# A thirteen-slot ring of expert weights, rows fetched per expert, and the smallest expert last, in a hybrid SSD/GLA/MoE layer

## The reference

```
scores = sigmoid(h2 @ w_router); biased = scores + router_bias
best   = argmax over the 4 groups of the sum of their two highest biased scores
idx    = top 2 of the 16 experts, inside the best group only
comb   = scores at idx, scaled to the sum 1, zero elsewhere
y_moe  = sum over e of comb[:, e] * ((silu(h2 @ wg[e]) * (h2 @ wu[e])) @ wd[e])
x = x + g2 * y_moe ;  y = rms_norm(x, final_norm_w)
```

## Time and profile before

| | |
|---|---|
| median of 3 runs | 1006.31 us |
| the profiled execution's own time | 1004.06 us |
| its span, first to last instruction | 1002.3 us |
| TensorE, VectorE, ScalarE, GpSimd busy | 94%, 44%, 23%, 14% |
| moved by DMA in all | 236.98 MB, mean 236 GB/s |
| GB/s in slices 31 to 38 of 40 | 387 419 419 420 417 420 420 421 |

### The profile page before, as it was taken

The page is one execution under the profiler, slowest core; times in us unless marked ns, Lnnn a source line. Parts: engine busy times, 40 slices in busy tenths (PEclk is TensorE's granted clock), DMA queues, the critical chain, the costliest instruction groups (busy, mean ns, idle before and its releaser), DMA issues.

```text
span 1002.3 us, 18836 instructions
## 1 busy us (share of the span) xinstructions
PE 944.0 (94%) x7702; PEld 659.7 (66%) x7702; DVE 441.4 (44%) x1094; ACT 233.2 (23%) x461; POOL 145.3 (14%) x236
## 2 busy tenths in 40 slices
PE   5999999999999999999999999999899988797895
PEld 2667666666666666666666777767599856564671
DVE  3221234676346986656641531134643342322316
ACT  2231222243263322232252300002231110110013
POOL 0000232343020343322300000011200000000010
PEclk9999999999999999999999999999999999899997
DMA  9943344564455655665443533342579999999973
GB/s 376 392 165 126 127 169 143 197 225 162 161 193 197 255 196 179 227 218 202 159 172 126 224 122 127 126 168 98 214 291 387 419 419 420 417 420 420 421 281 118
DMA packets 46541, 236.98 MB, mean 236 GB/s; under 512 B 6672, under 2 KB 10352, under 8 KB 23152
## 3 DMA queue, kind: packets, MB, share of 16 engines
q1 hardware_dynamic: 44480, 229.83, 59.7%
q0 software_dynamic: 1520, 5.34, 1.6%
q10 hardware_dynamic: 448, 0.50, 0.1%
HBM read 212.34 MB, written 23.31 MB: 235 GB/s over the span
## 4 chain that ended last, share of the span: by engine, by line
PE 73%; DMA 15%; DVE 6%; issue 2%; ACT 2%; SPq 1%; POOL 0%; POOLq 0%; DVEq 0%
PE pjB L884 15%; PE pjA L884 15%; DMA ring<-in_w 8%; PE pjA L1282 7%; PE pjB L1282 7%; DMA bp<-in_w 4%; PE states L1456 4%; PE states L1468 3%; PE states L1459 2%; DMA yd<-hF 2%; PE states L893 1%; PE bank L1019 1%; PE states L1261 1%; PE states L1019 1%; PE bank L1248 1%
## 5 line engine op out<-in xcount | busy, mean ns | idle before, releaser
L884 PE MATMUL pjA<-hF,ring 128*128 128x320 f32 x608 | 171.9, 436 | 0.5 <-ACT regA L1719 0.5
L884 PE MATMUL pjB<-hF,ring 128*128 128x320 f32 x608 | 171.8, 435 | 0.0
L884 PEld LDWEIGHTS pjA<-hF,ring 128*128 128x128 f32 x608 | 113.2, 190 | 50.7 <-issue 7.0
L884 PEld LDWEIGHTS pjB<-hF,ring 128*128 128x128 f32 x608 | 113.3, 190 | 48.6 <-issue 4.7
L1456 PE MATMUL states<-ring,oF 128*32 128x128 f32 x720 | 80.5, 273 | 2.1 <-DMA ring<-in_w 1.7
L1456 PEld LDWEIGHTS states<-ring,oF 128*32 128x32 f32 x720 | 78.0, 110 | 5.5 <-issue 2.7
L1459 PE MATMUL states<-ring,oF 128*32 128x384 f32 x720 | 80.7, 491 | 0.0
L2764 DVE TENSOR_TENSOR oF<-oF,states 128x256 f32<-128x256 f32 (+1 forms) x15 | 7.2, 483 | 139.9 <-PE states L1468 70.4
L2470 DVE TENSOR_TENSOR G<-G 128x320 f32<-128x320 f32 x32 | 47.1, 1510 | 0.0
L2076 POOL TENSOR_TENSOR G<-regA,G 128x128 f32<-128x128 f32 (+1 forms) x32 | 19.0, 594 | 192.3 <-ACT G L1775 192.3
L2173 POOL DMA_DIRECT2D yd<-hF x1 | 0.6, 640 | 244.2 <-DVE hF L2755 244.2
(11 more groups left out here) (565 smaller groups left out, 1518.2 us busy)
## 6 DMA issues: line engine op xcount, KB each, us to landing
ring<-in_w SPq DMA_DIRECT2D x144, 1024.0 KB, 8.5
rF<-in_w SPq DMA_DIRECT2D x11, 1024.0 KB, 18.6
bcF<-in_w SPq DMA_DIRECT2D x11, 1024.0 KB, 20.6
bp<-in_w SPq DMA_DIRECT2D x10, 1024.0 KB, 19.0
G<-in_ss SPq DMA_DIRECT2D x16, 512.0 KB, 4.7
out_ss_new<-G SPq DMA_DIRECT2D x16, 512.0 KB, 2.9
G<-csd SPq DMA_DIRECT2D x16, 320.0 KB, 3.5
G<-in_sg SPq DMA_DIRECT2D x4, 1024.0 KB, 6.4
```

Source lines behind the costliest of these rows:

```text
L884: mm = pe.matmul(pj[g % 2][:, 0:T], w[:, k, half * P:half * P + P], hF[:, k, :], start=(k == 0), stop=(k == KT - 1))
```

## The change

**Ring.** `SLOTS` goes from R + 3 to R + 7. The four new slots lie in xsF (two) and regA (two). Eleven chunks (`KNOWN`) are those of places 0 and 1 whose experts are known beforehand, without the last; they are asked for before the branch, number 11 in the branch as soon as the residual has been read out of regA, number 12 after the transposes of place 0's rows. Chunk order changes: gate and up of place 1 come before down of place 0.

**Rows per expert.** The 40 transposes of all rows, their copies and ScalarE's copy by offset go. SP loads each place's rows from `xd` to one of two buffers (`rows_in`), three places ahead, TensorE turns them (`turn_rows`, 8 transposes) between gate/up of place p and down of place p-1, ScalarE and VectorE copy 4 of the 8 tiles each. The `yd` writes move from SP to ScalarE's queue.

**Places.** `FULL_AT` is now 0, 1, 4, 6, 8, 10; `TINY_AT` 5, 9, 13 are places of up to 32 tokens, with `tiled_tiny` streaming 128 columns through each column group; the others hold 64, the last one too, which now gets the smallest expert. By the counts above places 0 to 15 hold 57, 31, 47, 44, 77, 27, 59, 40, 55, 25, 50, 36, 29, 18, 29 and 16 tokens.

**End.** The last expert's 16 tokens are finished apart: for up to 64 rows TensorE picks gate, residual and the other expert's contribution (`each_row`), VectorE and ScalarE norm them, and POOL scatters the finished rows over the ordinary ones in the output, after those have landed. For tokens 0 to 255 the residual is added by POOL, not VectorE.

The tables:

```diff
-SLOTS = R + 3
+SLOTS = R + 7
+KNOWN = R + 5
...
-FULL_AT = (0, 1, 2, 5, 8, 11, 14, 15)
-FIXED_AT = (0, 1, E - 1)
...
+FULL_AT = (0, 1, 4, 6, 8, 10)
+TINY_AT = (5, 9, 13)
+FIXED_AT = (0, 1)
```

SP, in the layer's last loads and then in the branch:

```diff
+                    sp.wait_ge(s_used, C_OUT)
+                    load_extra(3)
+                    load_extra(4)
...
+                sp.wait_ge(s_tm, 6)
+                sp.dma_start(slot(KNOWN), d["w"][chunk_row(*SEQ[KNOWN])]).then_inc(slot_ready(KNOWN)[0], 16)
                 sp.wait_ge(s_xd, 16 * 6)
-                sp.dma_start(xs01[:, 0, :], d["xd"][0:P, :]).then_inc(s_xe[0], 16)
-                sp.dma_start(xs01[:, 1, :], d["xd"][P:2 * P, :]).then_inc(s_xe[1], 16)
-                sp.wait_ge(s_oss, GH + 1)
-                sp.dma_start(hT, d["xd"][2 * P:XROWS, :].rearrange("(a p) c -> p a c", p=P)).then_inc(s_xe[1], 16)
...
+                rows_in(1)
+                sp.wait_ge(s_oss, GH + 2)
+                sp.dma_start(slot(KNOWN + 1), d["w"][weight_row(2) + SEQ[KNOWN + 1][1]]).then_inc(slot_ready(KNOWN + 1)[0], 16)
+                rows_in(2)
+                refill(0, 0, 4)
...
+                for p in range(3, LAST):
+                    refill(p, 0, 4)
+                    if p + 3 < E:
+                        rows_in(p + 3)
+                    refill(p - 1, 4, 6)
```

TensorE:

```diff
+                gate_up(0)
+                turn_rows(1)
+                gate_up(1)
+                turn_rows(2)
+                down(0)
+                turn_rows(3)
+                down(1)
+                gate_up(2)
+                for p in range(3, LAST):
+                    gate_up(p)
+                    turn_rows(p + 1)
...
+                    down(p - 1)
+                down(LAST - 1)
+                gate_up(LAST)
+                turn_act()
+                base_rows(0)
+                down(LAST)
+                base_rows(1)
+                base_rows(2).then_inc(s_gw, 1)
+                row_sums()
```

GpSimd, behind the six gathers:

```diff
+                for t in range(2):
+                    pool.wait_ge(s_gm, t + 1)
+                    pool.tensor_tensor(hT[:, t, :], hT[:, t, :], xT[:, t, :], ALU.add).then_inc(s_x3, 1)
+                pool.wait_ge(s_tix, 2)
+                pool.wait_ge(s_f, 4)
+                pool.wait_ge(s_out, 16 * 4)
+                pool.indirect_dma_start(out=d["yrows"], out_offset=bass.IndirectOffsetOnAxis(ap=tix[:, 0:1], axis=0),
+                                        in_=zF_, in_offset=None).then_inc(s_last, 16)
```

VectorE, the end:

```diff
+                summed(0).then_inc(s_gm, 1)
+                gated_up(LAST)
+                turned_last()
+                summed(1).then_inc(s_gm, 1)
+                cm(summed(2))
                 cm.wait()
...
+                dve.tensor_tensor(hT[0:NSAMP, 2, :], hT[0:NSAMP, 2, :], xT[0:NSAMP, 2, :], ALU.add).then_inc(s_base, 1)
+                final(0, 0, y2)
+                dve.wait_ge(s_gwc, 3)
+                weighted_half(0)
+                weighted_half(1)
+                final(1, 1, y2)
+                dve.wait_ge(s_zl, 2)
+                dve.wait_ge(s_gw, 2)
+                dve.tensor_tensor(zL, zL, b[4][:, :], ALU.add).then_inc(s_zl, 2)
+                final(2, 2, y2)
+                dve.wait_ge(s_zq, 2)
+                dve.reciprocal(zs[:, 1:2], zs[:, 1:2]).then_inc(s_frc, 1)
+                dve.wait_ge(s_frc, 4)
+                dve.scalar_tensor_tensor(zF_, zL, zs[:, 1:2], w2, ALU.mult, ALU.mult).then_inc(s_f, 1)
```

More of the change, by code:

```diff
@@ L821, in refills @@
                 of, row = None, None
[L822 to L827, removed]
+                for j in range(j0, j1):
+                    m = seq_of(p, j)
+                    if m in NEXT:
+                        q, i = SEQ[NEXT[m]]
+                        if q != of:
+                            of, row = q, weight_row(q)
+                        sp.wait_ge(s_used, C_MOE + m + 1)
+                        sp.dma_start(slot(NEXT[m]), d["w"][row + i]).then_inc(slot_ready(NEXT[m])[0], 16)
@@ L1470, in tiled_small, with tiled_tiny, gate_up @@
                 return mm
-            def gate_up(e, v, full=True):
-                he = heF[:, v]
+            def tiled_tiny(bank, rows, w, first, last):
+                for q in range(4):
+                    at = QUAD * q
+                    mm = pe.matmul(bank[at:at + QUAD, 0:P], rows(0), w[:, P * q:P * q + P], start=first, stop=last,
+                                   tile_position=(0, at), skip_group_check=True)
+                return mm
+            def gate_up(p):
+                he, tiles = heF[:, p % 2], tiled if p in FULL_AT else tiled_tiny if p in TINY_AT else tiled_small
+                if p:
+                    pe.wait_ge(s_hea, p)
+                    pe.wait_ge(s_heb, p)
                 for part, used in ((0, s_esg), (1, s_eac)):
-                    if not (isinstance(e, int) and e == 0):
-                        pe.wait_ge(used, e + 0)
+                    if p:
+                        pe.wait_ge(used, p)
                     for half in range(2):
-                        w = moe_chunk(pe, e, 2 * part + half)
+                        w = moe_chunk(pe, p, 2 * part + half)
                         for k in range(4):
@@ new lines, in base_rows, with row_sums @@
+                return mm
+            def row_sums():
+                pe.wait_ge(s_zq, 1)
+                for h in range(2):
+                    for half in range(2):
+                        mm = pe.matmul(b[0][SMALL * h:SMALL * h + SMALL, 0:1], ident[:, SMALL * half:SMALL * half + SMALL],
+                                       zs[:, 0:1], start=(half == 0), stop=(half == 1), tile_position=(0, SMALL * h),
+                                       skip_group_check=True)
+                mm.then_inc(s_gw, 1)
@@ L1599, in up @@
                     for part, used in ((0, s_sg), (1, s_au)):
-                        w = [moe_chunk(pe, e, 2 * part + half) for half in range(2)]
+                        w = [dense_chunk(pe, e, 2 * part + half) for half in range(2)]
                         for f in range(4):
```

676 lines of the change are left out of this document (333 added, 343 removed).

## The result

The changed kernel takes 1020.82 us in the median of 4 runs (1017.0 to 1024.55); the kernel before, measured again beside it, 1007.08 (1005.38 to 1008.71). The ratio is 1.0136, with a 95% interval of 1.0092 to 1.0181: slower by 13.7 us. The prediction was 995.5, a miss of 25.3 us. The profiled execution took 1017.0 us, its span is 1015.0.

The account below looks back on a forecast made before the run. The DMA weight stream was taken as the bound: last weight 10.0 us earlier, end 31.2 us instead of 31.9, together -10.7 us. From 1004.06 that makes 993.4; with 2.25 to the median, 995.5 was predicted, range 985 to 1003.

Parts of the forecast that it names:

- What must flow: Weight stream: chunks 11 to 95, fetched rows and results sum to 97.65 MB, 242.3 us at 0.403 MB/us.
- Start: Start of the branch's weight stream: chunk 11 issued at 715.8, data from 717.1 (715.7 to 719.6), 1 us of idle.
- the prediction's own signs of being wrong: Wrong if the stream doesn't start before 718 or the end behind the last gather is not 20 to 22 us.
- The two extra known chunks at nothing: Before the branch: two more 1 MB loads before 690 us cost nothing; without that cover 2 x 2.6 us.
- Rate and last weight: Weight stream: at 0.403 MB/us the last weight lands at 960.4, 10.0 us earlier.
- rival 1: Weight stream: engines stay even at 0.414 MB/us and TensorE's clock stays up, 986.6 us; chance 0.17.
- TensorE as cover: Weight stream: TensorE's work takes 220 of 242 us, so it stays beside the stream.
- Place 14's result: ScalarE's queue: issued at 947.1, 7.8 us and half a us for the second, landed at 955.3, gathers from 956.0.
- Rival 2: Place 14's result is no faster on ScalarE's queue, gathers 8.3 to 9.8 us later, about 1003.5 us; chance 0.11.
- The end: From the last weight to the end: 31.2 us instead of 31.9, output landed 987.5, scatter 991.4, span 991.6.
- The rule on the shared port: Residual additions at the end: POOL and VectorE pass each other; by the skill's contrary rule 4.3 us more, 999.8.
- Rival 3: Weight stream: TensorE becomes the bound as its clock falls; 1019 us with a quarter at half clock; chance 0.06.

Follow-up runs that it names:

- quarters: Changed kernel, but each place's rows are fetched as quarters of 256 columns over all 128 partitions, with 2 transposes per 32 rows: 994.1 us.
- low64: Changed kernel, but for places 5 to 15 each fetch brings 64 rows of 4 KB into partitions 0 to 63: 1021.8 us.
- mid64: Changed kernel, but for places 5 to 15 each fetch brings 64 rows of 4 KB into partitions 32 to 95: 997.0 us.
- q_ring11: Kernel with quarter rows fetched over 128 partitions, but a ring of 11 slots, without the two in regA: 994.9 us.
- q_ysp: Kernel with quarter rows over 128 partitions, but all places' results return to SP's queue, each behind the refills that follow its place: 999.3 us.
- q_vadd: Kernel with quarter rows over 128 partitions, but the end's residual additions of groups 0 and 1 go from GpSimd to VectorE: 994.5 us.
- all128: Changed kernel, but every fetch brings 128 whole rows of 4 KB into all 128 partitions, whatever the place needs: 1002.8 us.

## Why the prediction was wrong

**The step that failed is "What must flow".** The working put the fetched rows, 4.19 MB, into one sum with the weights and priced all bytes at the stream's 0.403 MB/us. That made 10.4 us for the rows. They cost 26.7 us more than this, the difference between the changed kernel and quarters. The rate was taken from a kernel whose loads all filled 128 partitions, and it holds for those: 419 GB/s with quarters. What the runs show in its place: a fetch into partitions 0 to 31, 0 to 63 or 0 to 95 slows the weights beside it, 341 ns a packet in the mean from 745 to 950 us for 312 with quarters, and 2.3 us for a fetch of 64 rows (low64 against mid64). The order rows ahead of the prediction showed the new shape (`regA<-xd 96x1024` where `hF<-xd 128x1024` had stood), and I read only its bytes. No rival had it either: the three doubted the queue, the engines' evenness and TensorE's clock, and none asked where the bytes land.

The other steps can be judged on quarters, which has the bytes, the queues and the order of the changed kernel. Its profiled execution took 994.02 us with a span of 992.1; 993.4 and 991.6 were predicted for the change. That it is so near is luck in part: the gathers began 1.5 us later than predicted (957.52 for 956.0), and the end behind them was 1.0 us shorter. (The prediction's last sum is off by 0.1: 993.4 and 2.25 make 995.6.)

- **Start.** Late, inside the bounds. Chunk 11 is issued at 718.05 in the changed kernel and 716.53 with quarters, for 715.8. Its data flow from 719.4 and 718.05 (packet records), for 717.1 and at most 719.6; both are past 718, one of the prediction's own signs of being wrong. The wait for the scatters ends at 723.7 and 722.5, not at 718.2. The last scatter is issued 2.5 and 1.2 us later than before, and the rest comes mostly from the load that now stands ahead of the wait, a collision that the sum left out: q_ring11 has no such load, and there the wait ends at 720.9, although its last scatter is issued at 716.1, after that of quarters (715.6). The share in 718 to 725 is 0.71 and 0.72, so about 2 us are idle there instead of 1.
- **The two extra known chunks at nothing.** SP's last ring load ahead of the branch starts at 692.35 (before 689.94), with quarters at 691.06, and place 0's first matmul at 719.48 and 717.96, against 718.35. Nothing that could be told from zero.
- **Rate and last weight.** Right with quarters. The last two weight loads are issued at 935.3 and 935.9 and land 24.2 to 26.1 us later, so at 960 to 962, for 960.4. The mean until 950 is 419 GB/s, but the share fades to 0.65 between 955 and 960, which I read as some engines being late again; rival 1 had the landing at 954 or earlier and is wrong.
- **TensorE as cover.** Right. Busy 179.16 of 205 us with quarters; I had 220 of 242, and the shares are 0.87 and 0.91.
- **Place 14's result.** Right. Issued at 972.11, the last of it landed 7.6 us later, 7.6 also with quarters (949.12); 8.2 were predicted. Rival 2 is wrong. I had not seen the larger part of what the queue saves, the buffer that comes free sooner (q_ysp).
- **The end.** Right in sum: 34.5 us behind the first gather for 35.6. The groups were weighted 7.3, 11.8 and 13.3 us after it, where 7.9, 12.6 and 14.1 stood. The scatter is last and waits for the output.
- **The rule on the shared port.** I read from the earlier trace rows that GpSimd and VectorE pass each other; that was wrong. Two operations beside each other took 3.35 us (2.34 for the other addition) and 3.29 us (1.22 alone), as the Trainium skill (SBUF — State Buffer, "Who interferes with whom") has it. Only one of the two additions met such an operation, 2.1 us instead of the 4.3 that I had worked out, and q_vadd shows that avoiding it wins nothing either.
- **Rival 3.** It has the sign of the result and not its mechanism: the granted clock fell to 0.90, but TensorE never bounded the stream: it was idle for 31.5 of the 205 us, with the DMA share at 1.02. With the fetches repaired the clock is 0.96, still with time to spare.

So the change with its rows fetched into all partitions is worth 13 us (quarters against 1007.27: ratio 0.9877, 0.983 to 0.9925), and one access pattern in it cost 26.7.

## What to carry to other kernels

Price a transfer in a full DMA stream by the partitions that it fills, too, not by its bytes alone: a small load into partitions 0 to 31, 0 to 63 or 0 to 95 holds up the large ones around it, while the engines look fully busy. In the changed kernel the weight packets around one such fetch lost 0.6 to 1.0, 1.3 to 2.0 and 1.7 to 2.1 us per DMA engine (packet records, places 5 to 15). Lay such a load out over all 128 partitions (rows cut in pieces, turned by transposes as before), or, where that can't be done, over partitions 32 to 95 or every second one, which did no harm here. When the DMA share is 1.0, read GB/s beside it, in stretches as short as one transfer, before believing that the stream runs at its rate.

## What the hardware showed beyond that

- The harm shows for writes into SBUF only. Results leave from 96 and 32 partitions, twice 64 (the first half from 0 to 63), or four times 32, all through the stage, and with quarters or all128 the rate beside them is 419 to 420 GB/s and a weight packet takes 312 ns.
- A fetch into all partitions costs its bytes even in a full stream, 8.6 us for 3.67 MB, and pieces of 1 KB do no harm that the times show (46 ns each, so four take 184, where a row of 4 KB takes 159).
- The long queue does no harm that shows. SP's single issues of weights take up to 7.57 us in the changed kernel with 13 slots, and with 11 slots nothing is won.
